# The factors of a head pair in 15 rounds of small steps, their GpSimd products on VectorE, and a shared tile one place later

## The reference, cut to what matters

```
w_log = -softplus(-(w0 + tanh(wd) @ w2)) - 0.5
decay = exp(-exp(w_log));  a = sigmoid(a0 + ad @ a2)
kk = k * k_k, normalised per head
k_dir = k * (1 + (a - 1) * k_a);  kka = kk * a
sa = S @ -kk
S = S * decay + sa * kka + v * k_dir;   y = S @ r
bonus = sum(r * mean(k_dir) * r_k) * v;  out = y + bonus
```

## Time and profile before

| | us |
|---|---|
| median of 3 runs | 3998.93 |
| lowest, highest | 3994.62, 4002.96 |
| the profiled execution | 3998.11 |
| its span, first to last instruction | 3996.3 |
| TensorE busy in it | 3696.5 |
| VectorE, ScalarE, GpSimd busy in it | 853.0, 652.6, 95.7 |

### The profile page before, as it was taken

How to read it: one execution, slowest core, us unless ns; L and a number is a source line. 1 busy time by engine, 2 the same in 40 slices (tenths; PEclk the granted TensorE clock), 3 DMA queues, 4 the chain that set the end, 5 groups by cost and what they waited for, 6 DMA issues and landing times. The chain is left out here.

```text
span 3996.3 us, 51934 instructions
## 1 busy us (share of the span) xinstructions
PE 3696.5 (92%) x23312; PEld 2196.4 (55%) x23312; DVE 853.0 (21%) x1976; ACT 652.6 (16%) x1474; POOL 95.7 (2%) x136
## 2 busy tenths in 40 slices
PE   8999999689888888898898899999999999999997
PEld 4444654433323333266777787888888444443454
DVE  1110521201111110134666213210000122101032
ACT  2110620100000000022343115022100001001231
POOL 0000000000000000000322000000000000000000
PEclk9999999799999999999999899999999999999999
DMA  6332011499999999920000210221212111120110
GB/s 247 117 137 84 22 43 42 168 428 428 426 425 424 426 426 427 427 105 1 4 3 4 101 43 12 95 77 64 84 64 84 63 63 64 63 84 32 45 64 21
DMA packets 113532, 593.51 MB, mean 149 GB/s; under 512 B 7296, under 2 KB 13056, under 8 KB 86944
## 3 DMA queue, kind: packets, MB, share of 16 engines
q1 hardware_dynamic: 113312, 590.20, 37.0%
HBM read 588.08 MB, written 2.10 MB: 148 GB/s over the span
## 5 line engine op out<-in xcount | busy, mean ns | idle before, releaser
L369 PE MATMUL banks<-slabs,ring 128*128 128x264 f32 (+2 forms) x5928 | 1802.8, 465 | 11.0 <-PEq L299 6.3
L369 PEld LDWEIGHTS banks<-slabs,ring 128*128 128x128 f32 (+1 forms) x5928 | 1127.3, 192 | 641.9 <-issue 512.6
L1794 PE MATMUL banks<-ring,slabs 128*64 128x512 f32 x3072 | 695.9, 602 | 115.8 <-DMA ring<-in_w_exp 103.4
L1794 PEld LDWEIGHTS banks<-ring,slabs 128*64 128x64 f32 x3072 | 220.9, 138 | 562.4 <-issue 427.4
L369 PE MATMUL banks<-ring,slabs 128*128 128x512 f32 (+3 forms) x560 | 158.4, 439 | 0.0
L1921 DVE TENSOR_TENSOR slabs<-slabs,banks 128x512 f32<-128x512 f32 x32 | 22.0, 688 | 512.4 <-PE banks L1794 512.4
L369 PEld LDWEIGHTS banks<-ring,slabs 128*128 128x128 f32 (+1 forms) x560 | 91.9, 188 | 69.8 <-issue 67.2
L2241 DVE TENSOR_TENSOR slabs<-banks,slabs 128x264 f32<-128x264 f32 x32 | 13.8, 433 | 487.9 <-PE banks L369 487.9
L2646 PE MATMUL banks<-ring 64*64 64x64 f32 (+1 forms) x2880 | 112.7, 229 | 1.4 <-issue 1.4
L1217 ACT ACTIVATE slabs<-slabs,small 128x513 f32<-128x513 f32 (+7 forms) x136 | 97.2, 714 | 90.3 <-DVE small L1173 90.2
L369 PE MATMUL banks<-ring 128*128 128x512 f32 x256 | 110.4, 593 | 0.0
(11 more groups left out here) (431 smaller groups left out, 2732.7 us busy)
## 6 DMA issues: line engine op xcount, KB each, us to landing
ring<-in_w_exp SPq DMA_DIRECT2D x192, 2048.0 KB, 15.8
ring<-in_w_in SPq DMA_DIRECT2D x19, 2048.0 KB, 10.6
ring<-in_w_ff SPq DMA_DIRECT2D x16, 2048.0 KB, 8.1
ring<-in_even_w_in SPq DMA_DIRECT2D x14, 2048.0 KB, 8.0
ring<-in_w_ada SPq DMA_DIRECT2D x12, 2048.0 KB, 8.6
ring<-in_w_out SPq DMA_DIRECT2D x4, 2048.0 KB, 7.9
ring<-in_even_w_out SPq DMA_DIRECT2D x4, 2048.0 KB, 7.8
ring<-in_w_proj_a SPq DMA_DIRECT2D x2, 2048.0 KB, 7.8
```

What stands on the lines that cost most here:

```text
L369: mm = core.nc.tensor.matmul(to, lhsT, rhs, start=kk0 + k < g, stop=kk0 + k >= kcs - g)
L1794: ins = mm(out[64 * c:64 * c + CAP, :], lhsT[:, k, :], w[:, at:at + 512], start=first and k == 0, stop=last and k == 3)
```

## The change

The steps of `Factors` are cut smaller and re-ordered, 15 in place of 13. The scans have a step each, the second one has the subtraction of the sums cut in two after it. ScalarE makes the first mix already in the step of the seventh gate, and its last two wide exponentials in a step of their own. VectorE makes the two products that were GpSimd's. `ready` is now sent after the last `BK` product and covers the `AR` products as well, so that `factors` is gone; a new `weighed` marks `t2`, for the bonus. A tile's second group on TensorE now waits for the values. In the list of tiles the shared one of pairs 2 and 3 comes after the fourth whole tile of pair 2 and not before it; that of pairs 0 and 1 stays.

```diff
-        self.rwkv = {k: count(f"rwkv_{k}") for k in ("gate_full", "gate_read", "padded", "cleared", "summed", "mixed", "powers", "factors", "ready",
+        self.rwkv = {k: count(f"rwkv_{k}") for k in ("gate_full", "gate_read", "padded", "cleared", "summed", "mixed", "powers", "ready", "weighed",
                                                      "bonus_full", "bonus_read", "values", "scan_full", "states", "taken", "step")}
...
             engine.wait_ge(core.rwkv["cleared"].sem, core.rwkv["cleared"].at(1))
-        if what in ("keys", "receptance"):
+        if what == "keys":
+            chunk(8)
+        if what == "unit_keys":
             engine.wait_ge(unit_keys.s["chunk"].sem, unit_keys.s["chunk"].at(1))
-            chunk(8)
         if what == "values":
...
+        if name == "dve":
+            engine.wait_ge(gates.s["chunk"].sem, gates.s["chunk"].at(8))
         if name == "pool":
...
         for p in range(0, pieces, 2):
-            order += [*whole(p)[0:3], [(p, SEQ, 1, 0), (p + 1, SEQ, 1, 1)], whole(p)[3], *whole(p + 1)]
+            order += [*whole(p), *whole(p + 1)]
+            order.insert(-5 if p == 0 else -4, [(p, SEQ, 1, 0), (p + 1, SEQ, 1, 1)])
         ends, through = [0] * pieces, [[0] * streams for _ in range(pieces)]
...
-PRE_STEPS = 13
+PRE_STEPS = 15
...
                     yield
-        for _ in range(3):
-            yield
-        pe.wait_ge(r["ready"].sem, r["ready"].at(p + 1))
+        for _ in range(5):
+            yield
+        pe.wait_ge(r["weighed"].sem, r["weighed"].at(p + 1))
         for s, (a, b) in enumerate(self.halves):
...
         T, icl = TOK2, self.icl
+        mix = lambda d, to: nc.scalar.activation(to, icl[:, d, 0:T], ACT.Identity, bias=self.one_less[:, w.m:w.m + 1], scale=w.col("k_a"))
         self.place_free("act", act)
...
                                          bias=core.col(bias, 4 * d + w.m)).then_inc(r["gate_read"].sem, r["gate_read"].add(1))
+                    if (j, d, s) == (1, 1, 0):
+                        if p:
+                            act.wait_ge(r["bonus_full"].sem, r["bonus_full"].at(2 * p))
+                        act.wait_ge(r["gate_read"].sem, r["gate_read"].at(8 * p + 6))
+                        self.inputs_ready("one_less", act)
+                        mix(0, self.t2).then_inc(r["mixed"].sem, r["mixed"].add(1))
                     yield
         act.wait_ge(r["gate_read"].sem, r["gate_read"].at(8 * p + 8))
-        if p:
-            act.wait_ge(r["bonus_full"].sem, r["bonus_full"].at(2 * p))
-        self.inputs_ready("one_less", act)
-        for d, to in enumerate((self.t2, self.t1)):
-            ins = nc.scalar.activation(to, icl[:, d, 0:T], ACT.Identity, bias=self.one_less[:, w.m:w.m + 1], scale=w.col("k_a"))
+        ins = mix(1, self.t1)
         ins.then_inc(r["mixed"].sem, r["mixed"].add(1))
...
         nc.scalar.activation(w.BK[:, :, 0, 0:T], w.AR[:, :, 1, 0:T], ACT.Exp, scale=-DECAY_SCALE).then_inc(r["taken"].sem, r["taken"].add(1))
+        yield
         nc.scalar.activation(w.AR[:, :, 0, 0:T], w.AR[:, :, 0, 0:T], ACT.Exp, scale=DECAY_SCALE)
...
         w, p, nc, r, T = self.w, self.p, self.core.nc, self.core.rwkv, TOK2
-        tt = nc.gpsimd.tensor_tensor
-        both_dirs = lambda t: t.unsqueeze(1).broadcast_to([P, 2, T])
         self.place_free("pool", pool)
...
         ins.then_inc(r["padded"].sem, r["padded"].add(1))
-        for _ in range(9):
-            yield
-        pool.wait_ge(r["powers"].sem, r["powers"].at(p + 1))
-        self.inputs_ready("receptance", pool)
-        tt(w.AR[:, :, 0, 0:T], w.AR[:, :, 0, 0:T], both_dirs(w.minus_kk), ALU.mult)
-        tt(w.AR[:, :, 1, 0:T], w.AR[:, :, 1, 0:T], both_dirs(w.r), ALU.mult).then_inc(r["factors"].sem, r["factors"].add(1))
-        for _ in range(4):
+        for _ in range(PRE_STEPS):
             yield
...
         blocks = lambda t: t.rearrange("p (b l) -> p b l", l=LB)
+        both_dirs = lambda t: t.unsqueeze(1).broadcast_to([P, 2, T])
         self.inputs_ready("constants", dve)
-        for _ in range(4):
-            yield
+        for _ in range(3):
+            yield
+        self.place_free("dve", dve)
         dve.wait_ge(r["padded"].sem, r["padded"].at(p + 1))
+        dve.wait_ge(r["gate_read"].sem, r["gate_read"].at(8 * p + 2))
+        step(nc.vector.tensor_tensor_scan(w.AR[:, 0, 1, :], goes_on, w.BK[:, 0, 1, :], 0.0, ALU.mult, ALU.add))
+        yield
         dve.wait_ge(r["gate_read"].sem, r["gate_read"].at(8 * p + 4))
-        nc.vector.tensor_tensor_scan(w.AR[:, 0, 1, :], goes_on, w.BK[:, 0, 1, :], 0.0, ALU.mult, ALU.add)
         step(nc.vector.tensor_tensor_scan(w.AR[:, 1, 1, ::-1], goes_on, w.BK[:, 1, 1, ::-1], 0.0, ALU.mult, ALU.add))
...
         nc.vector.tensor_copy(w.PC[:, 1, :], blocks(w.AR[:, 1, 1, :])[:, :, 0])
-        step(tt(w.AR[:, :, 0, :], w.AR[:, :, 1, :], w.BK[:, :, 1, :], ALU.subtract))
+        step(tt(w.AR[:, 0, 0, :], w.AR[:, 0, 1, :], w.BK[:, 0, 1, :], ALU.subtract))
+        yield
+        step(tt(w.AR[:, 1, 0, :], w.AR[:, 1, 1, :], w.BK[:, 1, 1, :], ALU.subtract))
         for d in range(2):
...
         yield
-        for _ in range(3):
-            yield
-        dve.wait_ge(r["mixed"].sem, r["mixed"].at(p + 1))
         self.inputs_ready("keys", dve)
-        tt(t1, t1, w.k, ALU.mult)
-        tt(t2, t2, w.k, ALU.mult)
-        step(nc.vector.scalar_tensor_tensor(out=icl[:, :, 0:T], in0=icl[:, :, 0:T], scalar=-1.0, in1=w.minus_kk.unsqueeze(1).broadcast_to([P, 2, T]),
+        dve.wait_ge(r["mixed"].sem, r["mixed"].at(2 * p + 1))
+        step(tt(t2, t2, w.k, ALU.mult))
+        yield
+        dve.wait_ge(r["gate_read"].sem, r["gate_read"].at(8 * p + 8))
+        dve.wait_ge(r["mixed"].sem, r["mixed"].at(2 * p + 2))
+        self.inputs_ready("unit_keys", dve)
+        step(nc.vector.scalar_tensor_tensor(out=icl[:, :, 0:T], in0=icl[:, :, 0:T], scalar=-1.0, in1=both_dirs(w.minus_kk),
                                             op0=ALU.mult, op1=ALU.mult))
+        yield
+        dve.wait_ge(r["taken"].sem, r["taken"].at(p + 1))
+        tt(w.BK[:, 0, 1, 0:T], t2, w.BK[:, 0, 0, 0:T], ALU.mult)
+        step(tt(t1, t1, w.k, ALU.mult))
+        yield
         dve.wait_ge(r["powers"].sem, r["powers"].at(p + 1))
-        tt(w.BK[:, 0, 1, 0:T], t2, w.BK[:, 0, 0, 0:T], ALU.mult)
+        tt(w.AR[:, :, 0, 0:T], w.AR[:, :, 0, 0:T], both_dirs(w.minus_kk), ALU.mult)
         step(tt(w.BK[:, 1, 1, 0:T], t1, w.BK[:, 1, 0, 0:T], ALU.mult))
         yield
-        tt(w.BK[:, :, 0, 0:T], w.BK[:, :, 0, 0:T], icl[:, :, 0:T], ALU.mult)
+        tt(w.AR[:, :, 1, 0:T], w.AR[:, :, 1, 0:T], both_dirs(w.r), ALU.mult)
+        tt(w.BK[:, :, 0, 0:T], w.BK[:, :, 0, 0:T], icl[:, :, 0:T], ALU.mult).then_inc(r["ready"].sem, r["ready"].add(1))
+        yield
         step(tt(t2, t1, t2, ALU.add))
+        nc.vector.scalar_tensor_tensor(out=t2, in0=t2, scalar=w.col("r_k"), in1=w.r, op0=ALU.mult,
+                                       op1=ALU.mult).then_inc(r["weighed"].sem, r["weighed"].add(1))
+        yield
         dve.wait_ge(r["values"].sem, r["values"].at(p + 1))
-        nc.vector.scalar_tensor_tensor(out=t2, in0=t2, scalar=w.col("r_k"), in1=w.r, op0=ALU.mult,
-                                       op1=ALU.mult).then_inc(r["ready"].sem, r["ready"].add(1))
-        yield
         for s, (a, b) in enumerate(self.halves):
...
                         pe.wait_ge(r["ready"].sem, r["ready"].at(last_piece(parts)))
-                        pe.wait_ge(r["factors"].sem, r["factors"].at(last_piece(parts)))
                     if i >= 1:
...
+                    if last_piece(parts):
+                        pe.wait_ge(r["values"].sem, r["values"].at(last_piece(parts)))
                     dve_read(1)
```

## The result

3969.72 us, median of 4 runs (3962.96 to 3974.35), beside 3999.88 for the kernel before in the same comparison: ratio 0.9925, 95% interval 0.9906 to 0.9943. That is 30 us faster, where 25 were forecast (3974), and inside the range of 3963 to 3987. The span of the profiled execution is 3966.5 us, 29.8 less.

What follows compares the result with a forecast made beforehand. TensorE's stalls on factor work in the dense stage and recurrence were taken as 39.2 us lost; less 0.1 and 14.1 left over, gain 25.0, from 3998.1 to 3973.1, median 3974 us. Range 3963 to 3987.

Steps and rivals of the forecast that it cites:

- ScalarE's shorter burst: Dense stage: with the exponentials split, ScalarE's burst ends 2.9 us sooner, helping end TensorE's 5.84 us wait.
- the shift at 2.0 us: Dense stage: VectorE's shift L2068 to L2071 takes 2.0 instead of 5.7 us without GpSimd's products beside it.
- the two units' later ask: Dense stage: TensorE asks for the bonus after unit 29, two units (7.6 us) later than in the kernel before.
- About 2 us per pair: GpSimd's products moved: VectorE about 2 us lighter per pair, 2.5 us more work against 4.5 us of slowing gone.
- masks held off by VectorE: VectorE's added products delay GpSimd's masks (L2807): at worst 5 us a pair, 3989 us; chance 0.04.
- Small steps: VectorE's factor work cut so its largest step is 2.5 us, not 8 to 9, hidden or nearly in level rounds.
- Stalls left: TensorE's waits for ScalarE's copies in pairs 1, 2, 3 shrink from 3.58, 4.08, 3.25 to 0.7, 1.2, 0.4 us.
- `ready` in the heavy rounds: Pairs 2 and 3, rounds where one tile ends and another begins: 3.0 us each for `ready`, bounds 0 to 4.5.
- The 2 us of lower clock: Recurrence: TensorE's lower clock after the two 3 us waits for `ready` costs 1 us each.
- The tile's move: Shared tile of pairs 2 and 3 one place later: changes no other count, costs nothing, else a 0.6 us copy.
- 1.2 us of low clock at the stage's start: Pair 1, recurrence's start: about 1.2 us of low clock that the change doesn't touch, within its 2.7 us left over.
- the rival of the heavy rounds: Recurrence: work only moves into heavy rounds, 9.9 us left in each of pairs 2 and 3; 3985 us; chance 0.09.

Runs made afterwards that it cites:

- e7: Kernel before with 15 rounds and only the bonus (TensorE's product, VectorE's step) two rounds later; 3988.1 us, ratio 0.9980, dense part 61.3 us.
- e1: Changed kernel with the two AR products made by GpSimd again; 3978.7 us, ratio 0.9939, stretch 378.7 us.
- e3: Changed kernel with ScalarE's last two wide exponentials back in the step of the first ones; 3981.0 us, ratio 0.9950, stretch 382.8 us.
- e2: Kernel before with only the two AR products moved from GpSimd to VectorE; 3989.2 us, ratio 0.9975, stretch 394.3 us.
- e6: Changed kernel with VectorE's small steps undone, six products in its step 10; 3983.1 us, ratio 0.9960, stretch 388.6 us.
- e5: Changed kernel with the product of AR[1] with r moved behind `ready`; 3970.4 us, ratio 0.9921, stretch 372.2 us.
- e10: The changed kernel itself, run again unaltered; 3970.1 us, ratio 0.9928, stretch 374.8 us.
- e4: Kernel before with only the shared tile of pairs 2 and 3 one place later; 3999.2 us, ratio 0.9996, recurrence 331.5 us.

## Why the prediction was right, and where not

**The whole.** 39.2 us of stalls were counted and 14.1 were to stay. The stretch says that 29.2 went. Sign, mechanism and the tile periods held. The surplus of 4.2 us, by the prediction's own terms: 1.2 in pair 1 (1.5 us left where 2.7 were to stay), 1.5 in pairs 2 and 3 (9.9 where 4.9, 4.5 and 2 were to stay) and 1.7 in the tiles with no factors at their side, less 0.2 in the dense stage.

**The dense stage: right size, wrong cause.** 8.5 us forecast, 8.3 measured. The prediction worked the wait away by ScalarE's shorter burst, by the shift at 2.0 us and by the two units' later ask, and had 0.4 us to spare. In the changed kernel L2536 ended just ahead of L2427 as forecast. But the later ask alone does it (e7, 61.3), and putting back GpSimd (e1, 62.2, with a wait of 0.88 us before the bonus) or the burst (e3, 61.7) costs next to nothing there. The step that credited them failed: they were cover that was hardly needed. The rows before tell as much: TensorE asked at 1865.28 - 5.84 = 1859.4 us, 7.6 us later is 1867.0, and L2522 had ended at 1865.2.

**GpSimd.** The mechanism holds both ways (e1, e2). About 2 us per pair were forecast; alone it is 7.5 us in the recurrence and 2.2 in the dense stage. On top of the other edits it is 3.9 in all, probably because small steps hide most of the slowing. The Trainium skill says (SBUF — State Buffer, "Who interferes with whom") that a VectorE instruction with two SBUF inputs contends with a GpSimd one that reads SBUF. E1's rows agree: 2.79 and 3.02 us where 0.7 and 1.26 are usual. The loss that could have come of it, masks held off by VectorE, didn't come: TensorE waits for no instruction of GpSimd anywhere in the stretch.

**Small steps** were treated as the condition for the rest and not priced. They are the dearest of the parts that were undone: without them 13.9 of the 29.2 us are lost (e6); what they bring alone was not run. What counts is how much VectorE has queued ahead of the signal that TensorE waits for, not how much it does.

**ScalarE.** Stalls left: 0.7, 1.2, 0.4 forecast, 0.92, 1.43 and none measured. One burst costs 8.1 us (e3), where the 2.1 us it adds three times would be 6.3; the rest is within the scatter.

**`ready` in the heavy rounds.** 3.0 us each taken from bounds of 0 to 4.5; measured 3.60 and 3.06. e5 shows that it is the queue ahead of it.

**The terms that were off.** The 2 us of lower clock behind those two waits: the clock did fall there, but not in every execution. The stretches right behind the 3.60 us wait and right behind the 3.06 us wait, first two in the changed kernel, then two in e10, the same kernel again (there the waits were 3.60 and 3.07), with columns as in the earlier trace rows, the clock third from the end:

```profile
2027.85:2032.00 4.15, 4.15 (x173) 4.15 (x176) 2.77 (x8) 0.00 (x0) 1.18 (x2) 0.59 0.01 4
2090.21:2095.00 4.79, 4.57 (x173) 4.44 (x175) 3.06 (x10) 0.00 (x0) 1.47 (x4) 0.69 0.01 3
...
2027.46:2031.61 4.15, 2.85 (x176) 2.72 (x176) 2.72 (x8) 0.00 (x0) 1.19 (x2) 1.00 0.01 4
2089.79:2094.58 4.79, 4.79 (x170) 4.79 (x172) 3.06 (x10) 0.00 (x0) 1.48 (x4) 0.56 0.02 7
```

Behind the first wait the low clock cost nothing that can be seen: the next 48 products of L2655 on `ring` began 5.76 us after the wait's end at 0.59, and 5.80 us after it at 1.00, where TensorE stood idle for 1.29 us for nothing that the profile shows. What it cost behind the second stays open, so no run bears the 2 us out. The tile's move was put at nothing and is perhaps 2.5 (e4). The two tiles with no factors at their side, said to stay, fell by 1.1 (43.76 to 42.69, and 42.70 in e10) and 0.6 us (the last, with the end of the stage); that is within the scatter and stays open. Pair 1 gained 5.7 us and not 4.5; it was given 1.2 us of low clock at the stage's start, which varies: from 1885 to 1890 us the clock was 0.50 in one execution and 0.92 in the other (e10), and the period took 50.93 and 49.53 us.

**Rivals.** By the prediction's own count (43.76 us for a tile, 5.7 and 1.9 for gates and scan) 1.5, 4.3 and 5.6 us of stalls are left in pairs 1, 2 and 3, the 2.84 us of the fifth period counted to pair 3; the rival of the heavy rounds had 9.9 for each of the last two. Over whole periods the clock did not fall but rose in every one with factors, from 0.82, 0.92 and 0.91 to 0.88, 0.99 and 0.98.

## What to carry to other kernels

Where engines work a fixed list round by round, a side job costs what it queues ahead of somebody's signal in one round, not its sum: cut it to what the main job leaves free in a round, and put the signal before the work nobody waits for yet. Before making an engine faster to end a wait, try asking later: asking two steps later did all of it in the dense stage. Elementwise work on GpSimd beside VectorE can cost more than all of it on VectorE: here 9.7 us of the stretch (e2).

## What the runs showed of the hardware

Two GpSimd products of 2.4 to 2.9 us stretched two VectorE products beside them to 2.79 and 3.02 us, for what takes 0.7 and 1.26; each ended 0.6 and 1.1 us after a GpSimd product did, a little under its own time alone. The shift L2068, which reads one large tensor and not two, was stretched too: 2.06 us before, 2.53 in e1, 0.49 alone. In the two executions of the changed kernel, behind waits of TensorE of 3.06 to 3.60 us, the granted clock over the next 4 to 5 us was 0.56, 0.59, 0.69 and 1.00, the 0.59 and the 1.00 behind the same wait of the same kernel; the stalls of 3.6 and then 2.4 us close together (pair 1 before) had left 0.60 over 12.9 us. At the start of the recurrence, after the same idle time of 3.09 us, the first 48 small matmuls took 1.56 us in one execution of the changed kernel and 1.03 in the other, and 0.93 in e1 and e5: the clock's level there is not settled by the program alone.
